# Low parts of the q, k and v weight pieces: made on GpSimd in twelve instructions of 128 columns instead of on VectorE in one

## What is computed

```
h  = rms_norm(x, ln_g) * (1 + scale) + shift            # 768 x 1024
qa, ka, va = h @ w_in[:, A columns]                     # 4 heads of 128 columns each
qb, kb, vb = h @ w_in[:, B columns]                     # 4 heads
qc, kc, vc = h @ w_in[:, C columns]                     # 3 groups x 4 heads
ya = diff_attention(rope(norm(qa)), rope(norm(ka)), va, lam)
yb = neighborhood_attention(norm(qb), norm(kb), vb, rpb)  # scores + relative-position bias, masked
yc = dilated_mixture(rope(norm(qc)), rope(norm(kc)), vc)
merged = sum over i of sigmoid(h @ G_i) * ((y_i * silu(h @ Z_i)) @ w_br[i])
x = x + gate * (merged @ w_out)
```

## Time and profile before

| | |
|---|---|
| median of 3 runs | 2300.53 us (2300.52 to 2300.61) |
| the profiled execution | 2298.62 us |
| its span, first to last instruction | 2296.8 us |
| TensorE busy | 2260.9 us, 98% |
| VectorE busy | 1720.7 us, 75% |
| ScalarE busy | 1115.9 us, 49% |
| GpSimd busy | 58.2 us, 3% |

### The profile page before, as it was taken

The page is one execution under the profiler, slowest core; times in us unless marked ns, Lnnn a source line. Parts: engine busy times, 40 slices in busy tenths (PEclk is TensorE's granted clock), DMA queues, the critical chain, the costliest instruction groups (busy, mean ns, idle before and its releaser), DMA issues.

```text
span 2296.8 us, 41721 instructions
## 1 busy us (share of the span) xinstructions
PE 2260.9 (98%) x15128; PEld 2124.0 (92%) x15128; DVE 1720.7 (75%) x4728; ACT 1115.9 (49%) x3059; POOL 58.2 (3%) x103
## 2 busy tenths in 40 slices
PE   7999999999999999999999999999999999999999
PEld 5888989999998999999888899899999989999998
DVE  7898888887886666676578867778887867676772
ACT  5667565444444544334357665744444353343340
POOL 0010120000000000000000102100000000000000
PEclk9999999999999999999999999999999999999999
DMA  7311321221111233321522111122211113332223
GB/s 288 116 49 67 115 91 70 96 94 61 56 45 50 82 113 121 101 97 61 169 81 82 52 68 45 58 84 87 76 35 58 48 47 109 108 117 93 88 95 117
DMA packets 78909, 200.28 MB, mean 87 GB/s; under 512 B 12273, under 2 KB 33393, under 8 KB 76913
## 3 DMA queue, kind: packets, MB, share of 16 engines
q1 hardware_dynamic: 62544, 171.87, 21.9%
q10 hardware_dynamic: 16160, 25.75, 3.1%
HBM read 176.59 MB, written 18.88 MB: 85 GB/s over the span
## 4 chain that ended last, share of the span: by engine, by line
PE 86%; DVE 7%; ACT 3%; issue 2%; DMA 1%; SPq 0%; ACTq 0%; DVEq 0%
PE ps_proj L1122 52%; PE ps_score L1166 11%; PE ps_pt L1166 8%; PE ps_pt L1315 2%; PE ps_score L1299 2%; PE ps_pv L1351 1%; PE ps_score L1283 1%; PE ps_pv L1332 1%; PE ps_tr L1365 1%; DVE top L2187 1%; PE ps_tr L1366 1%; PE ps_pv L1345 1%; ACT act_hi L1565 1%; ACT probs L1717 1%; DVE gained L2126 1%
## 5 line engine op out<-in xcount | busy, mean ns | idle before, releaser
L1122 PE MATMUL ps_proj<-w_hi,act_hi 128*128 128x384 f32 x1824 | 632.5, 347 | 5.8 <-DVE act_lo L2301 3.5
L1122 PE MATMUL ps_proj<-w_hi,act_lo 128*128 128x384 f32 x1824 | 612.2, 336 | 0.0
L1122 PE MATMUL ps_proj<-w_lo,act_hi 128*128 128x384 f32 x1824 | 611.9, 335 | 0.0
L1122 PEld LDWEIGHTS ps_proj<-w_hi,act_hi 128*128 128x128 f32 x1824 | 342.7, 188 | 10.7 <-ACT act_hi L1565 8.1
L1122 PEld LDWEIGHTS ps_proj<-w_lo,act_hi 128*128 128x128 f32 x1824 | 343.3, 188 | 0.0
L1122 PEld LDWEIGHTS ps_proj<-w_hi,act_lo 128*128 128x128 f32 x1824 | 342.5, 188 | 0.0
L1657 ACT ACTIVATE square<-ps_proj 128x256 f32<-128x256 f32 x228 | 88.1, 386 | 255.7 <-PE ps_proj L1122 255.5
L2120 DVE TENSOR_REDUCE ssq<-square 128x2 f32<-128x256 f32 (+1 forms) x228 | 95.5, 419 | 136.2 <-ACT square L1657 134.8
L2484 DVE TENSOR_TENSOR w_lo<-w_raw,w_hi 128x1536 fp32r<-128x1536 f32 (+3 forms) x105 | 169.5, 1616 | 11.2 <-ACT w_hi L1489 10.4
L1489 ACT ACTIVATE w_hi<-w_raw 128x1536 fp32r<-128x1536 f32 (+2 forms) x104 | 144.3, 1387 | 38.8 <-DMA w_raw<-in_w 20.2
L2397 DVE TENSOR_TENSOR s_lo<-s_raw,s_hi 128x512 fp32r<-128x512 f32 x224 | 150.9, 685 | 9.3 <-ACT s_hi L1820 7.5
(11 more groups left out here) (258 smaller groups left out, 5095.2 us busy)
## 6 DMA issues: line engine op xcount, KB each, us to landing
w_raw<-in_w SPq DMA_DIRECT2D x80, 768.0 KB, 5.7
s_raw<-in_w_gate SPq DMA_DIRECT2D x96, 256.0 KB, 3.2
strip<-in_w_strip SPq DMA_DIRECT2D x32, 512.0 KB, 6.6
w_raw<-in_w SPq DMA_DIRECT2D x24, 512.0 KB, 3.8
wb_raw<-in_w_branch SPq DMA_DIRECT2D x24, 512.0 KB, 4.0
first_ada<-in_w_first SPq DMA_DIRECT2D x8, 1024.0 KB, 13.1
w<-in_w_gate SPq DMA_DIRECT2D x32, 256.0 KB, 3.6
parked<-y_t ACTq DMA_DIRECT2D x4, 1536.0 KB, 5.1
```

The source lines that it names most:

```text
L1122: op = pe.matmul(out, sta[s](k), mov[m](k), start=(k == 0 and n == 0), stop=(k == chunks - 1 and n == 2))
```

## The change

For 72 of the 80 q pieces (all but the eight of `BY_NORM`) the subtraction `w_raw - w_hi` moves from VectorE's program to GpSimd's. VectorE made it in one instruction of 1536 columns; GpSimd makes it in twelve of 128 columns, the last of which raises a new semaphore `q_lo_ready`. It stands in GpSimd's program at the unit in which ScalarE makes the high part (`SPLIT_IN`), before the biases of the same unit. TensorE waits for `q_lo_ready` instead of `w_lo_ready` at these pieces. The z and output pieces and the first four pieces of each layer stay on VectorE.

```diff
-        w_lo_ready = tally("w_lo_ready", SPLIT_ORDER)
+        w_lo_ready = tally("w_lo_ready", [p for p in SPLIT_ORDER if p[0] != "q" or p in BY_NORM])
+        by_pool = [p for p in SPLIT_ORDER if p[0] == "q" and p not in BY_NORM]
+        q_lo_ready = tally("q_lo_ready", by_pool)
...
+            def low_part(p):
+
+                b = SLOT_OF[p]
+                pool.wait_ge(*w_hi_ready.at(p))
+                for c0 in range(0, PIECE, P):
+                    op = pool.tensor_tensor(w_lo[b][:, c0:c0 + P], w_raw[b][:, c0:c0 + P],
+                                            w_hi[b][:, c0:c0 + P].bitcast(F32), ALU.subtract)
+                op.then_inc(*q_lo_ready.inc(p))
+
             pool.wait_ge(later_in, 16 * 4)
             for n, u in enumerate(UNITS):
+                if n in SPLIT_IN and SPLIT_IN[n] in by_pool:
+                    low_part(SPLIT_IN[n])
                 if u[0] == "q" and u[5] == 5 and (u[2] == "B" or u[2:4] == ("A", 3)) and u[2:4] != ("B", 3):
                     biases(u[1], (u[3] + 1) % HEADS)
...
+            def lo_of(p):
+                return (w_lo_ready if p in BY_NORM else q_lo_ready).at(p)
...
                     if u[0] == "q" and u[5] == 0 and k == 3:
-                        pe.wait_ge(*w_lo_ready.at(pieces_of(u)[1]))
+                        pe.wait_ge(*lo_of(pieces_of(u)[1]))
...
                     if t == 0:
-                        pe.wait_ge(*w_lo_ready.at(pieces_of(u)[0]))
+                        pe.wait_ge(*lo_of(pieces_of(u)[0]))
...
-                if n in LOW_IN and not (u[0] == "z" and u[2] == "C") and u != output_unit(l, 0):
+                if n in LOW_IN and LOW_IN[n] not in by_pool and not (u[0] == "z" and u[2] == "C") and u != output_unit(l, 0):
                     low_part(LOW_IN[n])
```

## The result

| | before | after |
|---|---|---|
| median of four runs, us | 2300.53 | 2383.53 |
| lowest to highest, us | 2299.24 to 2300.61 | 2380.23 to 2386.22 |
| the profiled execution, us | 2298.62 | 2380.23 |
| its span, us | 2296.8 | 2378.4 |
| granted TensorE clock, mean | 1.00 | 0.985 |

The changed kernel takes 1.0366 times as long, with a 95% interval of 1.0354 to 1.0378: **83 us slower**. Slower was forecast, with 2402 us; the measured time lies within the range of 2362 to 2450. The experiments were run beside fresh executions of the kernel before, whose medians were 2299.43 to 2300.24 us; each ratio is to those.

A forecast was written before the change was run, and what follows sets the result against it. TensorE, with work for 98% of the span, was taken to bound the kernel; 81.4 (queue) + 7 (A) + 7 (C) + 6 (after the queue) = 101.4 us, added to the median, gave 2402 us, range 2362 to 2450.

The forecast's parts named there:

- The queue: At B2, B3 and C0g0 of each layer, pieces behind the last bias part come late on GpSimd: 81.4 us.
- The price of a piece: On GpSimd, twelve 128-column instructions at 0.437 us each, 5.25 us; range 0.30 to 0.51 us for each instruction.
- Nothing to catch up with: After the late pieces, TensorE works in B and C as before, without slack to make up lost time.
- The clock: TensorE's lower clock after idling, hidden between half 0 and half 1: counted 0, up to 1.8 us each (11 us).
- VectorE in A: A of layer 0, two pieces in each of three heads: 7 us lost; bounds 5.3 us won to 17.4 lost.
- a net load of 1.15 us for each piece: On VectorE, GpSimd's twelve instructions cost up to 2.9 us where 1.76 us were removed, loading it by some 1.15.
- VectorE in C: C1g1 and its like, eight places: 2.9 less 2.05 us of slack, 0.9 us each, 7 us; bounds 0 and 2.3 each.
- after the queue: In six places the second piece's twelve instructions run while VectorE catches up: some 1 us each, 6 us; bounds 0 and 17.
- twelve cost up to 2.9 us: Each GpSimd instruction costs the VectorE instruction it meets about 0.24 us, so a piece's twelve cost up to 2.9 us.
- GpSimd's busy time: Whole kernel: about 58 + 72 x 5.25 = 436 us.
- The rival of ports that bind everywhere: The port lock makes each of 60 unhindered pieces cost TensorE 1.15 us, 69 us in all: 2479 us; chance 0.09.
- The rival of relief: Pieces of B2, B3 and C0g0 come in time and A gains its idle 5.3 us: 2295 us; chance 0.03.

The follow-up runs named there:

- the experiment on the order: Changed kernel, all 72 pieces on GpSimd, each hindered pair's first piece ahead of bias part 0, its second between parts 1 and 2: 2305.73 us, 1.0022.
- the kernel of one long instruction: Changed kernel with one GpSimd subtraction of 1536 columns for each piece in place of twelve of 128: 2432.62 us, 1.0577.
- the kernel with memsets: Against the kernel with GpSimd's program reordered, each of GpSimd's twelve instructions writes zeros and reads nothing, leaving out the low parts: 2294.65 us, 0.9979.

## Why the prediction was right, and where its sum was off

- **The queue** was forecast at 81.4 us and cost 76.3. Place, number (six long waits, six short) and mechanism hold, and the experiment on the order shows it. The price of a piece, taken as 5.25 us, is 5.0 (10.00 us for both): 0.5 us in each place. At C0g0 I let 1.0 us of old waits go; there half 1 is 16.2 us late (379.05 - 26.26 - 336.61), and from it to the next unit t1 takes 2.41 us where it took 4.26, so 1.85 us went. 12.3 and 14.3 for 12.8 and 16.0.
- **Nothing to catch up with** behind a stall: right, the shift at B2 t5 is that at B2 t1.
- **The clock, counted 0:** right, and for the reason given. The 12 matmuls between the halves took 4.4 us, 4.6 were supposed; the cost in the open is 1.75 us a place, 1.8 were supposed.
- **VectorE in A:** 7 us were forecast for layer 0, 6.0 were found in both layers, 2.2 and 3.8. Two steps failed. The first is that only layer 0 was counted. In layer 1 TensorE did not wait for `y_tok` before, but waits now, 4.1 us in five places; in A of layer 0 it is 5.9 us in six. The second is the reason, a net load of 1.15 us for each piece. VectorE's busy time in A of layer 0 fell, from 114.11 us to 112.27, and TensorE lost 2.2 us all the same. What counts is the place: the subtraction that was taken away stood behind `y_tok`, and the lengthened instructions stand ahead of it. In A1 t3 (before, then after, where everything is 0.58 us early at the start of A1 t1) `y_tok` comes 1.2 us later in its unit:

```profile
88.44 0.40 DVE L2256 TENSOR_SCALAR y_tok<-ps_pv,rden,y_ss 128x128 f32<-128x128 f32 x1
88.77 1.75 DVE L2484 TENSOR_TENSOR w_lo<-w_raw,w_hi 128x1536 fp32r<-128x1536 f32 x1
```

```profile
89.08 0.41 DVE L2272 TENSOR_SCALAR y_tok<-ps_pv,rden,y_ss 128x128 f32<-128x128 f32 x1
```

  That 6.0 is near 7 is luck: one layer too few and too much for a piece nearly cancel. The reading of the earlier trace rows was loose too: the row shown there ends a wait for ScalarE's `qkv`, and of the 5.3 us of idle time in A only 2.3 us are put down to `y_tok`.
- **VectorE in C, 7 us, and after the queue, 6 us:** both are 0. The mis-sized term is "twelve cost up to 2.9 us": 0.24 us for each of the twelve. What came back in the whole kernel is 105 us for 864 instructions, 0.12 us each, or 1.46 us for a piece, which is less than the 1.76 us taken away. A meeting does cost as much as supposed. In the timeline of VectorE of after, in A1 beside GpSimd's twelve, these two last 0.56 and 0.42 us, against 0.28 and 0.15 in the kernel of one long instruction once GpSimd is done:

```profile
85.94 0.56 DVE L2170 TENSOR_TENSOR turned<-turned,crossed 128x128 f32<-128x128 f32 x1
86.41 0.42 DVE L2172 TENSOR_TENSOR newton<-newton,rstd 128x4 f32<-128x4 f32 x1
```

  But not every one of the twelve meets such an instruction: VectorE spends much of that time on sums and on PSUM reads, which don't lengthen (`ssq` 0.42 us, `gained` 0.41, with and without). The prediction counted softmax steps with these, and that is wrong: beside a piece `ntop` lasts up to 0.46 us for 0.17, and `probs` up to 0.58 for 0.35 in the new order. So `qk` in C was never later than its 2.05 us of slack allowed. At the queue's places VectorE was in fact held: one `qk` at B2 and one at B3 of each layer lasts 2.40 or 2.41 us, beginning beside GpSimd's 24 subtractions and ending 0.28 us behind the last of them. TensorE did not notice: it takes this one at 283.07, and the shift doesn't grow up to B2 t5:

```profile
274.55 2.41 DVE L2187 TENSOR_TENSOR qk<-gained,newton 128x256 f32<-128x256 f32 x1 [7.39 <-PE ps_tr L1382]
```

  In the sum, 13 of the 20 us that I was too high are this term, 5 the queue, 1 A, and 0.7 the program's start.
- **GpSimd's busy time** was forecast as 436 us and is 478.2. Beside VectorE a piece takes 5.60 or 5.86 us in A, up to 13.2 for two in C, and 10.0 for two at the places of the queue, where VectorE does little. That the hold works in both directions fits this. It cost nothing at 128 columns: TensorE waits for no other piece.
- **The rival of ports that bind everywhere** is refuted for 128 columns: its 60 pieces took in A's twelve, and those cost 6 us, the others nothing (the 60 made in B and C: 0.9999). With 1536 columns something of its kind and size came true: 75 us, of it some 28 in A, 6 in B and 42 in C.
- **The rival of relief**, 2295 us, comes near the 2294.65 us of the kernel with memsets, in part by luck: it took all of A's idle 5.3 us in layer 0, and A of layer 0 gave 2.9. It needs more than the queue mended. With the order alone right, 2305.73 us stay, since the reads of GpSimd take back what A would gain and leave 5.9 us of loss.

## What to carry to other kernels

Before giving an idle engine work, look at what stands ahead of it in that engine's program: its busy share of 3% said nothing, and a 1.6 us bias part that had to wait for a mask made 12 of 72 pieces late, 76 us in all. The cure was the order, not the amount; a wait of one consumer must not stand ahead of another's work that is due earlier. Work moved from VectorE to GpSimd gives VectorE back only what GpSimd doesn't hold it up for, here 22 of 127 us, and even that is no gain where the work taken away stood behind what others wait for and the delay falls ahead of it. How much is lost depends on the length of each GpSimd instruction: cut it short, but not so short that GpSimd itself comes late.

## What the runs showed of the hardware

- A GpSimd instruction that reads SBUF holds a VectorE instruction with two SBUF inputs to its end: 2.83 us for 0.43 beside one of 3.49 us. Beside back-to-back instructions of 128 columns VectorE mostly gets in after one and loses some 0.26 us at a meeting (a Newton step 0.42 us for 0.15). Not always: four `qk` in the changed kernel were held to the end of a run of subtractions, 2.4 us, and with 64 columns two `ntop` were held for 4.04 and 3.76. Why is open. The loss of the kernel is 75, 20 and 6 us for 1536, 256 and 128 columns.
- A GpSimd memset of 128 columns doesn't hold such an instruction (Newton steps at 153 ns). Twelve in a row do hold a VectorE `TENSOR_SCALAR` of 256 columns from SBUF to SBUF, for 1.50 us where it takes 0.35 alone. A long subtraction holds the same instruction for 3.35 us.
- GpSimd's subtraction takes 0.415 us from start to start for 128 columns where VectorE does little (10.00 us for 24); one of 1536 columns takes 3.42 to 3.90, 3.54 in the mean.
- After the six waits of 8.63 to 15.49 us for GpSimd, TensorE's matmuls of 384 columns started every 0.32 us; at B2 t0 the granted clock was 0.50 there, the lower level, 1.2 GHz. At B2 t0 of layer 0 they started every 0.17 us again soon after half 1 began, with the clock at 1.00.
